# A hybrid encoder block on one core: router products moved behind the output products, and the first expert tile's rows made by TensorE

## What is computed

```python
for l in range(DEPTH):
    h = rms_norm(x, g_mix[l])
    x = x + mixer(h, w_in[l], ..., w_out[l], rel_bias[l])
    h = rms_norm(x, g_ffn[l])
    x = x + hier_moe(h, w_group_router[l], b_group_router[l], w_expert_router[l],
                     b_expert_router[l], w_e_gate[l], w_e_up[l], w_e_down[l])
return rms_norm(x, g_final)
# hier_moe: 36 logits per token (4 group, 32 expert), then for the two chosen experts
#   silu(h @ w_gate) * (h @ w_up) @ w_down, each weighted by its probability
```

## Time and profile before

| | us |
|---|---|
| median of three timed runs | 670.78 |
| the profiled execution, its own time | 679.34 |
| its span, first to last instruction | 677.5 |
| PE busy | 573.9 (85%) |
| DVE busy | 342.7 |
| POOL busy | 296.1 |
| ACT busy | 257.6 |
| mean granted TensorE clock | 0.942 |

### The profile page before, as it was taken

How to read it: one execution, slowest core, us unless ns; L and a number is a source line. 1 busy time by engine, 2 the same in 40 slices (tenths; PEclk the granted TensorE clock), 3 DMA queues, 4 the chain that set the end, 5 groups by cost and what they waited for, 6 DMA issues and landing times.

```text
span 677.5 us, 12329 instructions
## 1 busy us (share of the span) xinstructions
PE 573.9 (85%) x4305; PEld 385.9 (57%) x4308; DVE 342.7 (51%) x847; ACT 257.6 (38%) x445; POOL 296.1 (44%) x470
## 2 busy tenths in 40 slices
PE   3899999999999999999998308799989859696882
PEld 2577788876665777777888204444445424243430
DVE  4418999999988993478131581211211201111145
ACT  6444433246565746533224003334333323232222
POOL 5434434479996213355810026445445442525221
PEclk9999999999999998999997557999999989999997
DMA  9222724232202033034068986999899999999863
GB/s 296 64 69 63 249 62 119 68 91 74 71 15 63 1 124 125 1 125 155 1 249 282 412 319 222 406 409 408 312 403 409 408 409 408 408 402 399 326 260 124
DMA packets 59118, 149.23 MB, mean 220 GB/s; under 512 B 8836, under 2 KB 25220, under 8 KB 59086
## 3 DMA queue, kind: packets, MB, share of 16 engines
q1 hardware_dynamic: 53582, 139.89, 55.5%
q0 software_dynamic: 5360, 8.41, 3.5%
q10 hardware_dynamic: 144, 0.52, 0.2%
HBM read 145.37 MB, written 12.60 MB: 233 GB/s over the span
## 4 chain that ended last, share of the span: by engine, by line
PE 53%; DVE 21%; SPq 11%; DMA 6%; issue 4%; ACT 3%; POOL 1%; DVEq 0%; POOLq 0%; ACTq 0%
PE bank L689 26%; PE bank L958 10%; SPq L416 8%; PE bank L975 5%; DVE bm L1386 4%; DVE m L1385 4%; DVE conv_buf L1377 3%; DMA gates<-in_w_e_up 3%; PE bank L767 2%; SPq L426 2%; PE bank L902 2%; PE bank L931 2%; DMA region<-expert_rows 2%; PE bank L800 1%; PE bank L788 1%
## 5 line engine op out<-in xcount | busy, mean ns | idle before, releaser
L689 PE MATMUL bank<-h_hi,w_part 128*128 128x512 f32 (+1 forms) x528 | 173.4, 398 | 3.2 <-DVE h_lo L1335 1.7
L538 POOL TENSOR_TENSOR w_part<-region,w_part 128x1024 fp32r<-128x1024 f32 (+1 forms) x52 | 109.9, 2114 | 147.5 <-ACT w_part L1040 147.5
L689 PEld LDWEIGHTS bank<-h_hi,w_part 128*128 128x128 f32 (+1 forms) x528 | 98.0, 186 | 30.4 <-issue 6.8
L958 PE MATMUL bank<-region,kT 128*32 128x256 f32 x1536 | 93.7, 398 | 16.2 <-DMA region<-in_w_e_up 12.0
L1702 DVE TENSOR_TENSOR mask_b<-mask_b,bank 128x128 f32<-128x128 f32 x30 | 8.7, 288 | 188.3 <-ACT mask_b L1288 113.1
L689 PE MATMUL bank<-h_lo,w_part 128*128 128x512 f32 (+1 forms) x264 | 103.0, 390 | 0.0
L958 PEld LDWEIGHTS bank<-region,kT 128*32 128x32 f32 x1536 | 56.1, 115 | 61.0 <-issue 37.3
L1040 ACT ACTIVATE w_part<-region 128x1024 fp32r<-128x1024 f32 (+1 forms) x52 | 48.0, 925 | 108.1 <-PE bank L689 107.9
L588 POOL TENSOR_TENSOR carrier<-mhalf 128x1 f32<-128x1 f32 x185 | 34.0, 201 | 123.8 <-ACT qT L1295 108.6
L1420 DVE SCALAR_TENSOR_TENSOR bank<-glu,cv,bank 128x256 f32<-128x256 f32 x196 | 78.6, 479 | 0.0
L975 PE MATMUL bank<-region,mask_b 128*32 128x512 f32 x384 | 46.2, 598 | 11.3 <-DVE mask_b L1705 11.3
(11 more groups left out here) (273 smaller groups left out, 882.5 us busy)
## 6 DMA issues: line engine op xcount, KB each, us to landing
region<-in_w_e_down SPq DMA_DIRECT2D x22, 1024.0 KB
region<-in_w_e_gate SPq DMA_DIRECT2D x44, 512.0 KB
region<-in_w_e_up SPq DMA_DIRECT2D x44, 512.0 KB
region<-in_w_in SPq DMA_DIRECT2D x16, 1024.0 KB, 6.1
gates<-in_w_e_gate SPq DMA_DIRECT2D x20, 512.0 KB
gates<-in_w_e_up SPq DMA_DIRECT2D x20, 512.0 KB
conv_buf<-in_w_e_down SPq DMA_DIRECT2D x10, 1024.0 KB
region<-in_w_out SPq DMA_DIRECT2D x2, 2048.0 KB, 7.9
```

Source lines behind the costliest of these rows:

```text
L538: g.tensor_tensor(unit_part(u, 1), unit_raw(u), unit_part(u, 0).bitcast(F32), ALU.subtract)\
L689: last = mm(out_, a_parts[p], b_parts[q], start=start and x_ == 0, stop=stop and x_ == 2)
L958: last = mm(bank[0][32 * c:32 * c + 32, 0:FF], xTs[:, k, at_:at_ + 32], w_gu[slot][:, e, :, half, k, j * P:(j + 1) * P], start=(half == 0 ...
```

## The change

**Router.** The router no longer works on the normed rows. Each block's residual rows x_rows are transposed, and g_ffn is multiplied into the router's weights (DVE, the five operations that make wr); the row's scale comes in when DVE adds the bias, in four operations in place of one. 28 of the 32 transposes stand between output products, the last four behind the products of blocks 0 to 2. ACT copies seven of the eight groups to bm, kT and v_rows, DVE the eighth, ahead of block 3's norm. All 32 router products come behind the last output product. conv_buf is free of the transposed rows.

**First tile.** DVE makes, right behind the ranks, a matrix first_hit of 0 and 1 (token by slot of the first pair's first tile) in two operations. PE multiplies h2row with it: 32 products of 64 columns give the transposed rows of tile 0, with no gather. Both halves are copied by ACT. POOL's gathers begin with tile 1. The placement matrix moves: col_w is built by five operations of 512 elements in place of three, at the same point of DVE's program; the transposes and the copy stand at the end.

**Loads.** Down weights of sets 1 and 2 are issued behind the first half of the output product. The gate and up weights of set 2, which overwrite h2row, wait for xg_mm 2, the end of the first tile's products. The router's weights are loaded behind piece 9 of w_in, in runs of 4 to 32 bytes: 8 x 128 runs in each of six loads.

**End.** late_rows(0) stands ahead of weighted_row(1), the banks of the last products are in another order, and DVE takes row 0's norm ahead of later additions.

```diff
-                    sp.dma_start(wr_g[:], w_gr[0].rearrange("(p k) g -> p k g", k=KD)).then_inc(ld_router, 16)
-                    sp.dma_start(wr_e[:], w_er[0].rearrange("g (p k) e -> p g (k e)", k=KD)).then_inc(ld_router, 16)
+                if p == 9:
+                    with nc.allow_non_contiguous_dma(reason="router weights by rows"):
+                        sp.dma_start(wr_g[:], w_gr[0].rearrange("(k p) g -> p k g", k=KD)).then_inc(ld_router, 16)
+                        for gr in range(NG):
+                            sp.dma_start(wr_e[:, gr, :, :], w_er[0, gr].rearrange("(k p) e -> p k e", k=KD))\
+                                .then_inc(ld_router, 16)
+                        sp.dma_start(gffn_T[:], g_ffn.rearrange("a (k p) -> p (a k)", k=KD)).then_inc(ld_router, 16)
...
                 load_expert(0, pair_at(0), 0, half)
+            sp.wait_ge(S["unit_mm"], WO1)
+            load_down(1, pair_at(1))
+            load_down(2, pair_at(2))
             sp.wait_ge(S["wo_mm"], TB)
             for half in range(2):
                 load_expert(0, pair_at(0), 1, half)
...
                 sp.dma_start(h2_dram[b * P:(b + 1) * P, :], h2row[:, b, :]).then_inc(st_h2, 16)
             for half in range(2):
                 load_half(1, pair_at(1), half)
-            load_down(1, pair_at(1))
 
             sp.wait_ge(st_h2, 16 * TB)
-            sp.wait_ge(S["x2_mm"], 2 * TB)
+            sp.wait_ge(S["xg_mm"], 2)
             for half in range(2):
                 load_half(2, pair_at(2), half)
-            sp.wait_ge(S["rt_mm"], 1)
-            load_down(2, pair_at(2))
...
 
-            gather(0, 0)
             gather(1, 1)
-            pool.wait_ge(gathered[0], 16)
-            hold(2, S["rows_ready"])
             gather(2, 2)
-            gather(3, 3)
             pool.wait_ge(gathered[1], 16)
             hold(3, S["rows_ready"])
-            pool.wait_ge(S["xg_ready"], 1)
...
+
+            def merged_rest(b, units):
+
+                for u in units:
                     if b == 0:
                         pe.wait_ge(S["w_lo"], u + 1)
                     for kk in range(2):
                         last = merged_products(1, b, u, kk)
-                last.then_inc(S["wo_mm"], 1)
-
...
+                if u == NUNIT - 1:
+                    last.then_inc(S["wo_mm"], 1)
+
+            def transpose_x2(b, hf):
+
+                turn = x2_turns.index((b, hf))
+                pe.wait_ge(S["wo_ev"], TB * hf + b + 1)
...
+                for kk in range(4):
+                    k = 4 * hf + kk
+                    last = tr(bank[6 + turn % 2][:, kk * P:(kk + 1) * P], xr[:, b, k * P:(k + 1) * P], ident[:])
+                last.then_inc(S["x2_mm"], 1)
...
+            rest = range(WO1, NUNIT)
+            merged_rest(0, rest)
+            transpose_x2(0, 0)
+            transpose_x2(1, 0)
+            merged_rest(1, rest)
+            transpose_x2(0, 1)
+            transpose_x2(2, 0)
+            merged_rest(2, rest[0:2])
+            transpose_x2(3, 0)
+            transpose_x2(1, 1)
+            merged_rest(2, rest[2:4])
+            merged_rest(3, rest[0:1])
+            transpose_x2(2, 1)
+            merged_rest(3, rest[1:4])
             pe.wait_ge(S["wr_ready"], 1)
             pe.wait_ge(S["wo_ev"], TB)
-            transpose_rows(h2row, S["h2_ready"], S["x2_mm"], S["x2_ev"], (6, 7), router_logits)
+            for b in range(TB):
+                for hf in range(2):
+                    if (b, hf) == (TB - 1, 0):
+                        transpose_x2(TB - 1, 1)
+                    router_logits(b, hf)
...
+
+            pe.wait_ge(S["xg_ready"], 1)
+            pe.wait_ge(S["h2_ready"], TB)
+            pe.wait_ge(S["x2_ev"], 2 * TB)
+            for k in range(KD // 2):
+                for half in range(2):
+                    for b in range(TB):
+                        rows = h2row[:, b, half * BANK:(half + 1) * BANK].rearrange("p (q k) -> p k q", k=KD // 2)
+                        to = bank[6 + k // 2][:, k % 2 * P:(k % 2 + 1) * P].rearrange("p (e u n) -> p u e n", e=2, u=2)
+                        last = mm(to[:, half, :, :], rows[:, k, :], first_hit[:, b, :, :],
+                                  start=(b == 0), stop=(b == TB - 1))
+                if k % 2:
+                    last.then_inc(S["xg_mm"], 1)
...
-            pe.wait_ge(S["col_ready"], 1)
-            for b in range(TB):
-                last = tr(bank[5][:, b * P:(b + 1) * P], col_w[:, b, :], ident[:])
-            last.then_inc(S["place_mm"], 1)
-            pe.wait_ge(S["x2_ev"], 2 * TB)
-            transpose_tile(0)
...
+            pe.wait_ge(S["col_ready"], 1)
+            for b in range(TB):
+                last = tr(bank[5][:, b * P:(b + 1) * P], col_w[:, b, :], ident[:])
+            last.then_inc(S["place_mm"], 1)
             pe.wait_ge(S["diagw_ready"], 1)
...
             weighted_row(0)
+            pe.wait_ge(S["yev_a"], early + 3)
+            pe.wait_ge(S["place_ev"], 1)
+            late_rows(0)
             weighted_row(1)
-            pe.wait_ge(S["yev_a"], early + 3)
-            late_rows(0)
             late_rows(1)
...
+
+            def x2_out(turn):
+
+                act.wait_ge(S["x2_mm"], turn + 1)
+                a(x2_T(turn), bank[6 + turn % 2][:], ACT.Copy).then_inc(S["x2_ev"], 1)
+
+            x2_out(0)
+            x2_out(1)
+            x2_square(0)
+            x2_out(2)
+            x2_out(3)
+            x2_square(1)
+            x2_out(4)
+            x2_out(5)
+            x2_square(2)
+            x2_out(6)
+            x2_square(3)
...
-            act.wait_ge(S["place_mm"], 1)
-            a(place, bank[5][:], ACT.Copy).then_inc(S["place_ev"], 1)
             rows_T(0)
+            act.wait_ge(S["xg_mm"], 2)
+            a(xTs[:, 2:4, :].rearrange("p k n -> p (k n)"), bank[7][:, 0:2 * P], ACT.Copy).then_inc(S["xtev_v"], 1)
+            act.wait_ge(S["col_ready"], 1)
             for b in range(TB - 1):
                 last = a(diag[:, b, :], ident[:], ACT.Copy, scale=wts[:, 1, b:b + 1])
...
+            act.wait_ge(S["place_mm"], 1)
+            a(place, bank[5][:], ACT.Copy).then_inc(S["place_ev"], 1)
...
             for b in range(TB):
                 dve.wait_ge(S["wo_mm"], b + 1)
                 residual(1, b)
+                if b == TB - 1:
+                    dve.wait_ge(S["x2_mm"], 2 * TB)
+                    v.tensor_copy(x2_T(2 * TB - 1), bank[7][:]).then_inc(S["x2_ev"], 1)
                 mean_square(1, b)
...
             dve.wait_ge(S["rank_mm"], 1)
+            ranks = bank[2][:, 0:TB * NE].rearrange("p (b e) -> p b e", b=TB)
+            e0 = 2 * pair_at(0)
+            link(v.scalar_tensor_tensor(hic[:].rearrange("p (b e) -> p b e", b=TB), ranks[:, :, e0:e0 + 2], 1.0,
+                                        Mb[:, :, e0:e0 + 2], ALU.add, ALU.mult))
+            v.tensor_tensor(first_hit.rearrange("p b e n -> p (b e) n"), spread(iota[:, 1:SLOTS + 1], 1, 2 * TB),
+                            spread(hic[:], 2, SLOTS), ALU.is_equal).then_inc(S["xg_ready"], 1)
...
-            link(v.tensor_tensor(col_hit, spread(col_code, 1, 2 * TB), spread(hic[:], 2, P), ALU.is_equal))
-            link(v.tensor_tensor(col_hit, col_hit, spread(wts[:, :, :].rearrange("p c b -> p (c b)"), 2, P), ALU.mult))
-            v.tensor_tensor(col_w, col_hit[:, 0:TB, :], col_hit[:, TB:2 * TB, :], ALU.add)\
-                .then_inc(S["col_ready"], 1)
+            for c in range(2):
+                link(v.tensor_tensor(col_hit, spread(col_code, 1, TB), spread(hic[:, c * TB:(c + 1) * TB], 2, P),
+                                     ALU.is_equal))
+                link(v.tensor_tensor(col_hit if c else col_w, col_hit, spread(wts[:, c, :], 2, P), ALU.mult))
+            v.tensor_tensor(col_w, col_w, col_hit, ALU.add).then_inc(S["col_ready"], 1)
...
-            dve.wait_ge(S["rows_ready"], 1)
-            v.tensor_copy(xg, ring[:, 0, :]).then_inc(S["xg_ready"], 1)
-            rows_T(0)
...
-            for b in range(3):
+            for b in range(2):
                 add_row(b, 0)
             for k in range(2):
                 add_late(k)
+            add_row(2, 0)
+            mean_square(2, 0)
             add_row(3, 0)
+            dve.wait_ge(ld_gbc, 32)
+            scale_out(0, whole)
             for k in range(2, 4):
                 add_late(k)
             add_row(3, 1)
-            mean_square(2, 0)
-            dve.wait_ge(ld_gbc, 32)
-            scale_out(0, whole)
-            for k in range(4, 6):
-                add_late(k)
             mean_square(2, 1)
             scale_out(1, whole)
-            for k in range(6, 8):
+            for k in range(4, 8):
                 add_late(k)```

On PE, from the end of the output product to the first expert tile, before (L674 and L902 are router transposes and products, L914 to L916 the ranks, L921 the table, L937 the placement matrix, L931 the first tile's rows):

```order
L674 MATMUL bank<-ident,gates 128x128 x16
```

67 lines of the change are left out of this document (36 added, 31 removed).

## The result

The changed kernel takes 669.35 us (median of 20 runs, 668.28 to 672.39). The kernel before, in 20 runs beside it, took 678.1 us (668.95 to 681.81). The ratio is 0.9899, 95% interval 0.9879 to 0.9918: 1.0% faster, less than the 2% that the prediction called distinguishable. The forecast was 659.8, with a range of 652 to 669, so the time lies 9.6 us above the forecast and 0.35 us above the range. The *gain*, on the other hand, was forecast as 11.0 us and came out as 9.0 between the two profiled executions (679.34 and 670.38; spans 677.5 and 668.6). Most of the miss is in what the gain was taken from.

What follows compares the result with a forecast made beforehand. Two chains from router to end, TensorE's tiles and the expert weight stream, were taken as the bound. Tiles -9.2 and end -1.8 gave -11.0: 679.34 to 668.3, less 8.6 for the base, 659.8; range 652 to 669.

Steps and rivals of the forecast that it cites:

- the last of the sum: Whole kernel: profiled execution taken as 8.6 us above the timed median 670.78, lowering the forecast from 668.3 to 659.8.
- Router, -5.2: Router stage: transposes moved into the output product, products partly at full clock; end at 372.3 instead of 377.53, -5.2 us.
- VectorE's chain, +0.95: DVE from logits to table: extra operations for logits and first_hit delay the table's operands by 0.95 us.
- First tile's products, +2.05: TensorE ahead of the table: 64 passes take 13.8 us, until 394.0, so the table waits 2.05 us.
- Index table to tile 1, -7.0: From index table to tile 1's start: 13.4 us in place of 20.4, ACT being late next; -7.0 us.
- rival B: Clock low in tile 1: gate products take 6.38 in place of 3.66; 4.5 us lost, 664.3; chance 0.20.
- The stream: Expert weight loads: 10 us rest before set 2, place 3 at 405.0 instead of 414.0; -9 us, no cap.
- End, -1.8: Kernel's end: late_rows(0) one weighted row earlier, row 0's norm fills a wait; -1.8 us, 0 to 3.
- Router weights, 0: Router's fine loads behind piece 9: 400 packets take 10 us, piece 10 in by about 135, in time; 0 us.
- rival C: Router's fine loads hold up piece 10 of w_in: 32 us of stall, +21 us, 692; chance 0.06.
- A: Clock stays up through router and first tile's products: router ends at 369.0, 16.4 us gain, 654.4; chance 0.20.
- D: First tile's rows not early: 0.35 us a pass, ending at 402.6; 8.6 us of gain lost, 668.4; chance 0.10.

Runs made afterwards that it cites:

- e1: The kernel before, run again unchanged; 680.58 us, ratio 1.000 to the kernel before.
- e2: The kernel before with its one-column variance products spread two behind each group of three dense products over the next two branch units; 675.48 us, ratio 0.9953.
- e14: The changed kernel with the normed rows' columns permuted, so the first tile's 64 products read 128 neighbouring columns as weights; 669.91 us.
- e4: The changed kernel with 14 dense products behind the router's last product and 3 behind the rank products, results dropped; 671.10 us.
- e12: The changed kernel with the 14 and 3 dense products, the first tile's products reading neighbouring columns, giving wrong rows; 665.33 us (one run).
- e15: The changed kernel with the normed rows' columns permuted and the 14 and 3 dense products added; 665.88 us.
- e5: The changed kernel, run again unchanged; 669.79 us, ratio 0.9864 to the kernel before.
- e13: The changed kernel, run a third time unchanged; 670.94 us, ratio 0.9921 to the kernel before.
- e11: The changed kernel with the end restored to the order of the kernel before; 671.17 us, ratio 0.9905 to the kernel before.
- e18: Repeat of the changed kernel with the first tile's rows gathered and transposed as in the kernel before, without the 64 products; 671.25 us.
- e3: The changed kernel with the one-column variance products spread over the next two branch units; 675.38 us, ratio 0.9916 to the kernel before.
- e16: The changed kernel with permuted columns, dense products, half of set 2's weights issued early and ScalarE's diagonals behind the tile loop; 665.60 us.

## Why the prediction was right or wrong, point by point

**The step that failed is the last of the sum.** "It lies 8.6 us above the median of the timed runs, 670.78; taken off there the forecast is 659.8." The profiled execution was the typical one. The median of three was not: in 20 runs the median is 678.1, and 17 of them lie at 675.9 or above. e1 shows that an execution of 678 needs no fall in the branch stage, and on the two chips where their clocks are on record the runs of 669 to 672 are those with the highest. Without that step the forecast would have been 668.3, 1.0 us under the result. Part of that nearness would have been luck: the change's own part of the gain is 7.0 us and not 11.0, and 1.9 us came from before 338 us, where it does nothing. The 4.0 us too much are 1.1 for the tiles, 1.8 for the end and 1.7 that the stream lost behind place 7's release, less 0.6 gained between tile 1 and that release. A profiled execution whose clock is known is a better base than three times that differ by 9 us among themselves; or the range had to take in both bases.

**Router, -5.2.** It ended 8.0 us earlier, of which 1.9 came from before 338 us. So -6.1. Its parts were as taken: the 28 transposes moved the output product's end by 3.2 us (3.6 taken), the clock fell 4.4 us behind it (4.0), and from there to the router's end it took 10.1 us (10.7). That the old router would itself take 6.8 us less at full clock (19.4 and 12.6 us, e2) is not in the prediction.

**VectorE's chain, +0.95.** The index table came 3.5 us earlier: -8.0, +3.6 for the table's wait, so +0.9 is left for this. Right.

**First tile's products, +2.05.** The step that was mis-sized: 15.20 us, not 13.8, and the table waited 3.6 us. The nearest row, the router's 0.215 a pass, has neighbouring columns as weights; the step of four columns adds 0.02 us at half clock (e14) and 0.12 at full clock (e4, e12, e15).

**Index table to tile 1, -7.0.** 409.07 - 395.19 = 13.9 us in place of 20.4: -6.5. The diagonals and the table load were late next, as forecast; the gather of tile 1 (7.7 us to its landing) was as late as these. Clock low in the lead-in (down products 2.69 us in place of 1.92) was rival B in part; tile 1 itself ran at full clock in this execution, in 4.23 us in e5.

**The sum for the tiles** was -9.2, and measures -10.0 with the 1.9 from before, -8.1 without.

**The stream** rested where the prediction said (382 to 394), place 7 was released at 475.73 (forecast near 477), with 2 us of rest still ahead of it. But "if both start earlier by X, the end comes earlier by X" is too simple: -10.6 us at that release became -8.9 at the end. After 478 the stream took longer for the same bytes: from 582 to 602 it moved 384 GB/s at a share of 1.00, where before had 404.

```profile
582.00:602.00 20.00, 16.18 (x234) 8.87 (x234) 2.74 (x8) 5.55 (x9) 8.23 (x25) 1.00 1.00 384
```

That is 1.0 us of the 1.7; the rest I can't place. It varies between executions: e5, the same kernel, moved 404 GB/s in that stretch, was released at 477.65, 1.9 us later, and ended at the same 668.6. Why the rate dips in one and not in the other I did not test.

**End, -1.8.** From the loads of the expert rows to the last instruction 33.4 us in place of 34.9; but e5, e13 and e11 (old order) have 35.4, 34.4 and 34.7. Counted from SP's load behind the last expert weights (g_final, 632.93 before and 623.99 after) both profiles take 44.6 us to the last instruction, and e11 45.0. So the 8.9 us are all there before the end begins, and no gain of the end is shown.

**Router weights, 0.** Right, rival C did not come: the loads stand at 116 to 122 us and were in by 125; from 25 to 266 us ScalarE's splits of the weights stand 1.3 us later than before throughout, with no step at the loads.

**The rivals.** A: the clock did not stay up in the changed kernel's router, but did in e2's; and its 6.9 us for the first tile's products at full clock would have been wrong, since these took 0.2375 us a pass at either clock. D's mechanism (a higher price a pass) held in its small form, 15.2 in place of 22.4 us.

**What the prediction did not see** is that two of its parts stand for each other. It booked the first tile's rows as -7.0 + 2.05 and the early down weights as what keeps the stream from capping them. Undoing the down weights alone costs 4 us; with the first tile's products undone as well, it costs 0.8 us beside e18, no more than repeats differ.

## What to carry to other kernels

Before a difference is put on a base, ask what tells the base's own runs apart: three times that spread by 1.4% with a clock that differs from run to run are no base, and the mean granted clock, recorded with each run, says which is which. Where two chains end together (tiles and weights here), price each edit with the other chain held still: an edit on one gave nothing, edits on both 2 to 5 us; and undo the parts of a change in pairs, not only one by one. Read the access pattern of an operand before its price is taken from a row of the same size.

## What the runs showed of the hardware that I had not expected

- A product of 64 f32 columns behind 128 weight columns read with a step of four (16 bytes) takes 0.2375 us at a granted clock of 1.00 (e4, some 12 products) and of 0.50 (after). With neighbouring columns it takes 0.115 us at 1.00 (e12, e15) and 0.2175 at 0.50 (e14, 13.92 / 64).
- The transposes of v_rows read with that step too. Four took 0.74 us, their weight loads 0.210 us each in the median (after); with neighbouring columns 0.66 and 0.140 (e15).
- The clock falls at different distances behind dense work in one and the same stretch: behind the output product's end 3 us (e3), 4.4 us (after), 5 us (before), 13 us (e2). 14 dense bf16 products of 512 columns took 4.6 to 5.6 us from a low clock, and it was 1.00 at their end (e4, e12, e15, e16).
- In stretches of 4 us from 560 to 608 the changed kernel's queues moved 357 GB/s (share 0.97) to 413 (1.02), and from 582 to 602 two executions of it moved 384 and 404 GB/s.
